# Dilated attention: the query's square sums behind three slabs, one group each, in place of all six among the scores

## What is computed

```python
q = (h @ w_q).reshape(bsz, seq, 3, 16, 64)
q = _rms(q, q_gain[:, None, :]) * 64 ** -0.5
...
s = jnp.einsum('birhd,bjrhd->bhrij', qb, kb) + biases[g]
s = jnp.where(valid, s, -jnp.inf)
```

## Time and profile before

| What | Value |
|---|---|
| Time, median of 3 runs | 2720.44 us (2717.47 to 2721.78) |
| The profiled execution | 2737.34 us |
| Its span in the trace | 2735.2 us |
| Mean granted clock of TensorE | 0.973 |
| TensorE busy (matmuls) | 2615.1 us, 96% |
| VectorE, ScalarE busy | 1762.1 us (64%), 1313.4 us (48%) |
| Dilated attention | about 2194 to 2535 us of the span |

### The profile page before, as it was taken

How to read it: one execution, slowest core, us unless ns; L and a number is a source line. 1 busy time by engine, 2 the same in 40 slices (tenths; PEclk the granted TensorE clock), 3 DMA queues, 4 the chain that set the end, 5 groups by cost and what they waited for, 6 DMA issues and landing times.

```text
span 2735.2 us, 60697 instructions
## 1 busy us (share of the span) xinstructions
PE 2615.1 (96%) x23300; PEld 2545.4 (93%) x23300; DVE 1762.1 (64%) x2831; ACT 1313.4 (48%) x1947; POOL 74.4 (3%) x106
## 2 busy tenths in 40 slices
PE   7997999899999999999989999699999999999999
PEld 7996887899999999989989998689999999999999
DVE  5657565566756757766657656867667565555774
ACT  5544433355545546555445445345555454454552
POOL 0000442000000000000000000000000000000000
PEclk9999997899999999999999999899999999999999
DMA  5554200344555655445545645126655564452564
GB/s 197 188 185 130 94 3 33 109 154 153 190 188 179 202 194 183 158 139 184 192 146 184 206 155 165 43 98 199 206 173 196 179 183 123 135 141 95 170 209 144
DMA packets 114321, 424.24 MB, mean 155 GB/s; under 512 B 12433, under 2 KB 19044, under 8 KB 113796
## 3 DMA queue, kind: packets, MB, share of 16 engines
q1 hardware_dynamic: 105696, 408.99, 45.3%
q10 hardware_dynamic: 8484, 13.30, 2.3%
HBM read 421.12 MB, written 1.12 MB: 154 GB/s over the span
## 4 chain that ended last, share of the span: by engine, by line
PE 91%; DVE 3%; ACT 2%; issue 2%; DMA 0%; ACTq 0%; POOL 0%; DVEq 0%; SPq 0%; POOLq 0%
PE bank L462 21%; PE bank L464 21%; PE bank L463 21%; PE bank L396 5%; PE bank L397 4%; PE bank L398 4%; PE bank L2186 2%; PE bank L1605 1%; ACT hi L339 1%; PE bank L1580 1%; PE bank L443 1%; PE bank L444 1%; PE bank L445 1%; PE bank L1189 1%; PE bank L2114 1%
## 5 line engine op out<-in xcount | busy, mean ns | idle before, releaser
L347 DVE TENSOR_TENSOR lo<-raw,hi 128x1024 fp32r<-128x1024 f32 (+1 forms) x728 | 936.6, 1294 | 419.8 <-ACT hi L339 418.2
L339 ACT ACTIVATE hi<-raw 128x1024 fp32r<-128x1024 f32 (+1 forms) x728 | 787.4, 1106 | 361.3 <-PE bank L398 184.2
L462 PE MATMUL bank<-Hh,hi 128*128 128x256 f32 x3120 | 875.9, 281 | 18.4 <-DVE lo L347 18.1
L463 PE MATMUL bank<-Hl,hi 128*128 128x256 f32 x3120 | 874.3, 280 | 0.0
L464 PE MATMUL bank<-Hh,lo 128*128 128x256 f32 x3120 | 874.3, 280 | 0.0
L462 PEld LDWEIGHTS bank<-Hh,hi 128*128 128x128 f32 x3120 | 591.7, 190 | 21.4 <-DVE lo L347 20.4
L463 PEld LDWEIGHTS bank<-Hl,hi 128*128 128x128 f32 x3120 | 592.2, 190 | 0.0
L464 PEld LDWEIGHTS bank<-Hh,lo 128*128 128x128 f32 x3120 | 590.1, 189 | 0.0
L464 PE MATMUL bank<-Ah,lo 128*128 128x256 f32 x1408 | 394.0, 280 | 0.0
L463 PE MATMUL bank<-Al,hi 128*128 128x256 f32 x1408 | 393.9, 280 | 0.0
L462 PE MATMUL bank<-Ah,hi 128*128 128x256 f32 x1408 | 393.9, 280 | 0.0
(11 more groups left out here) (414 smaller groups left out, 4164.5 us busy)
## 6 DMA issues: line engine op xcount, KB each, us to landing
raw<-in_w SPq DMA_DIRECT2D x600, 512.0 KB, 3.4
raw<-in_w SPq DMA_DIRECT2D x128, 704.0 KB, 4.2
dB<-dil_bias ACTq DMA_DIRECT2D x16, 384.0 KB, 10.0
X<-in_x SPq DMA_DIRECT2D x2, 512.0 KB, 5.3
mem_x<-in_mem ACTq DMA_DIRECT2D x1, 1024.0 KB, 4.7
gWS<-in_ws ACTq DMA_DIRECT2D x1, 1024.0 KB
gBS<-in_bs ACTq DMA_DIRECT2D x1, 1024.0 KB
out_x<-X SPq DMA_DIRECT2D x4, 256.0 KB, 2.6
```

Of the source, the lines that this page charges most:

```text
L339: act.activation(k.hi[:, q, :w], k.raw[:, q, :w], ACT.Copy).then_inc(k.hi_ready, 1)
L347: dve.tensor_tensor(k.lo[:, q, :w], k.raw[:, q, :w], k.hi[:, q, :w].bitcast(F32), ALU.subtract).then_inc(k.lo_ready, 1)
L462: pe.matmul(out, wh, xh, start=first, stop=False)
L463: pe.matmul(out, wh, xl, start=False, stop=False)
```

## The change

The sums leave the scores. A new method `pe_query_sums(pe, c, g)` runs the sums of one group, and is called behind q1 (i = 4) for group 0, behind q2 for group 1 and behind v0 for group 2, there in front of the even unit's scores. They are written to bank 3 from column 256 on, not from column 0. ScalarE squares each group by itself, behind its split at i = 3, 4 and 5, once VectorE has evicted that q slab; the square waits for the same group's sums of the pair before. TensorE waits for the square of the group that it sums, and for the key's scales in front of group 0. The query's scales wait for the sums of group 2.

```diff
--- before.py
+++ after.py
@@ -1497,8 +1497,10 @@
                     self.pe_transposes(pe, 2 * c - 1)
                 if c >= 2 and i == 5:
                     self.pe_heads(pe, c - 2)
+                if 4 <= i <= 6:
+                    self.pe_query_sums(pe, c, i - 4)
                 if i == 6:
-                    self.pe_scores(pe, 2 * c, sums=True)
+                    self.pe_scores(pe, 2 * c)
                 if c and i == 7:
                     self.pe_output(pe, 2 * c - 1)
 
@@ -1555,7 +1557,19 @@
                 ins = pe.transpose(out, self.VF[:, g, half * P:(half + 1) * P], k.ident)
         k.pe_done.done(ins, f"d.vt{c}")
 
-    def pe_scores(self, pe, u, sums=False):
+    def pe_query_sums(self, pe, c, g):
+
+        k = self.k
+        k.act_done.wait(pe, f"d.qsq{c}.{g}")
+        if g == 0:
+            k.act_done.wait(pe, f"d.rk{c}")
+        for half in range(2):
+            at = T + 2 * (GROUPS * half + g)
+            ins = pe.matmul(k.bank[3][:, at:at + 2], self.QSQ[:, g, (1 - half) * P:(2 - half) * P], k.sel[:, 0:2],
+                            start=True, stop=True)
+        k.pe_done.done(ins, f"d.qs{c}.{g}")
+
+    def pe_scores(self, pe, u):
 
         k, c, e = self.k, u // 2, u % 2
         k.dve_done.wait(pe, f"d.k{c}")
@@ -1565,18 +1579,8 @@
         else:
             pe.wait_ge(k.rstd_ready, self.sh.norm_n["pe"])
         f, z = slice(e * HEAD, (e + 1) * HEAD), c % 2
-        if sums:
-            k.act_done.wait(pe, f"d.qsq{c}")
-            k.act_done.wait(pe, f"d.rk{c}")
         for g in range(GROUPS):
             b, o = 4 + g // 2, (g % 2) * T
-            if sums:
-                for half in range(2):
-                    at = 2 * (GROUPS * half + g)
-                    ins = pe.matmul(k.bank[3][:, at:at + 2], self.QSQ[:, g, (1 - half) * P:(2 - half) * P], k.sel[:, 0:2],
-                                    start=True, stop=True)
-                if g == GROUPS - 1:
-                    k.pe_done.done(ins, f"d.qs{c}")
             pe.matmul(k.bank[b][:, o:o + T], self.Q[z][f, g, :P], self.K[z][f, g, :], start=True, stop=True)
             ins = pe.matmul(k.bank[6][:, g * P:(g + 1) * P], self.Q[z][f, g, P:], self.K[z][f, g, :P], start=True, stop=True)
         k.pe_done.done(ins, f"d.s{u}")
@@ -1651,9 +1655,11 @@
                     self.act_load(act, c + 1)
                 if c and i == 4:
                     self.act_probabilities(act, 2 * c - 1)
-                if i == 5:
-                    k.dve_done.wait(act, f"d.qraw{c}")
-                    d(act.activation(self.QSQ[:], self.Q[c % 2][:], ACT.Square), f"d.qsq{c}")
+                if x == "q":
+                    act.wait_ge(k.banks_freed, RING + s + 1)
+                    if c:
+                        k.pe_done.wait(act, f"d.qs{c - 1}.{g}")
+                    d(act.activation(self.QSQ[:, g, :], self.Q[c % 2][:, g, :], ACT.Square), f"d.qsq{c}.{g}")
                 if c >= 2 and i == 5:
                     self.act_heads(act, c - 2)
                 if i == 6:
@@ -1692,9 +1698,9 @@
     def act_query_scales(self, act, c):
 
         k = self.k
-        k.pe_done.wait(act, f"d.qs{c}")
+        k.pe_done.wait(act, f"d.qs{c}.{GROUPS - 1}")
         r = self.RQ[:, c % 2].rearrange("p h g e -> p (h g e)")
-        k.act_done.done(act.activation(r, k.bank[3][:, :12], ACT.Ln, bias=k.col(C_EPS), scale=1.0 / HEAD), f"d.lq{c}")
+        k.act_done.done(act.activation(r, k.bank[3][:, T:T + 12], ACT.Ln, bias=k.col(C_EPS), scale=1.0 / HEAD), f"d.lq{c}")
         k.act_done.wait(act, f"d.lq{c}")
         k.act_done.done(act.activation(r, r, ACT.Exp, scale=-0.5), f"d.rq{c}")
```

## The result

Over 19 runs of each kernel the median is 2704.03 us with the change and 2715.24 us without. The ratio of the times is 0.993, 95% interval 0.9909 to 0.995, so the change is worth 19 us (13.6 to 24.7) of 2715. (The two medians alone lie 11.2 us apart, under that interval; why they differ from the ratio the record doesn't show.) I had forecast 15.2. The median lies in my range; the ratio on 2715.24 gives 2696.2, just under its lower end. Of the 9.0 us between that and my 2705.2, 3.8 are a larger gain than forecast and 5.2 a lower start: I had built on 2720.44, the median of three runs.

What follows compares the result with a forecast made beforehand. The prediction took TensorE to bound the kernel, busy for 2615.1 of 2735.2 us. Its terms, -13.0 - 3.0 + 0.8 = -15.2 us, took the median 2720.44 to 2705.2 us, range 2698 to 2714.

Steps and rivals of the forecast that it cites:

- What bounds, and the cause of the fall: TensorE sets the pace; its clock halves behind even units' scores because of the long mixture of sums and scores, 4.16 us.
- Rival A: At the scores, the clock doesn't hang on the sums: all falls stay, 2718.2 us, chance 0.10; in part, 0.05.
- Rival B: Behind q1's slab, transposes meeting sums bring new falls in 7 pairs, making it slower: 2729.5 us, chance 0.05.
- C: Rival: TensorE gains, but VectorE or ScalarE becomes late and eats it; no chance of its own, counted in the width.
- (1) Clock: Behind the even units' scores the clock stays at 2.4 GHz, saving 13.0 us, bounds none to 13.6 us.
- 27.2 us are eight of them: Half-clock time behind the scores counted as eight pieces of 3.4 us, each costing 1.62 us, 13.0 us in all.
- The start of the sum: Forecast counted from the runs' median 2720.44 us, taking off the same 15.2 us as from the profiled execution.
- (2) Moved sums: Sums between slabs take 0.54 us a group, saving 0.38 us a pair, 3.0 us in all, bounds 0 to 3.0.
- (3) Squares: ScalarE's three squares for one cost it 3.4 us in all, hidden under its waits for TensorE: taken as zero.
- (5): Sums written to columns 256 to 267 of bank 3 add no instruction and cost nothing.
- (4) The wait in pair 0: TensorE waits some 0.8 us once for the square of q0 behind two DMA issues, bounds 0 to 1.0 us.

Runs made afterwards that it cites:

- e2_wide: Kernel before, order kept, each sum with a moving operand of 128 columns instead of 2: no fall, dilated attention 332.3 us, whole time 0.9979.
- e6_triple: Changed kernel with group 0's sums done three times over behind the transposes of q1: dilated attention 336.6 us, one fall, in pair 0.
- e8_after: Changed kernel, nothing altered, profiled once more: dilated attention 329.0 us with one window at half clock, whole time 0.9933 of the kernel before.
- e1_block: Kernel before with a pair's six sums in one block in front of the even unit's scores: five windows, dilated attention 333.2 us, whole time 0.9967.
- e12_squares: Kernel before with three squares of 256 columns for one of 768, sums still among the scores: dilated attention 340.5 us, seven windows at half clock.
- e7_before: Kernel before, nothing altered, profiled a second time: dilated attention 350.2 us with 12 windows of 3.4 us at half clock.
- e5_twogroups: Changed kernel with group 0's sums behind q2, groups 1 and 2 in front of the even unit's scores: dilated attention 326.4 us, one fall.

## Why the prediction was right or wrong

**What bounds, and the cause of the fall: right.** The falls at the scores went with the sums, and e2_wide shows that without sums of few columns there is none. Why twelve such loads bring it beside scores and not behind transposes (e6_triple) stays open. Rival A is out: none stays at the scores. By the rule of the Trainium skill (TensorE: Matmul & The Clock Gate, HAM oscillation — how this bites in real kernels), gaps in which TensorE is idle make it fall. The piece behind the wait of 2.1 us in pair 0 of e8_after goes that way, though the page speaks of longer gaps, and a wait of 1.9 us in the first profile brought none. Those of the earlier trace rows don't agree, since they stand behind 3.50 of 3.50 us busy. Rival B is out too (e6_triple): the transposes that the same page of the Trainium skill (Part 4: PE-mode transpose) says don't engage the full clock didn't lose it here, with sums behind them. So is C: no new wait of TensorE but that for the square of q0.

**(1) Clock: the step that failed.** The price of a window holds roughly: with 1.62 us each, four profiles of the kernel before come to between 328.9 and 329.8 us, once the 1.0 us of wait is taken off one. (I had read it against pair 1. Against pair 3 of the changed kernel, where the same slab takes from 2291.64 to 2294.58, 2.94 us, it is 1.53; between pairs of e1_block it is 1.7.) What failed is "27.2 us are eight of them". I read the number off one execution, and allowed 2 us either way. Four have 8, 12, 11 and 11 windows. The mean of 10.5 makes the term 17.0 us, not 13.0: 4.0 us too little, outside the 2 that I had allowed.

**The start of the sum: too high.** "I put the same difference on the median" set the time on the 2720.44 us of three runs; 19 gave 2715.24. These 5.2 us are no part of the change, and more than the 3.8 by which the gain was missed. Either miss alone stays inside my range: 2715.24 - 15.2 is 2700.0, and 2720.44 - 19 is 2701.4.

**(2) Moved sums: too small a gain.** I took 0.54 us for a group between slabs and noted that no row showed it. It is 0.44 to 0.45 for the groups behind slab or transposes, 0.54 in front of scores: 1.43 us a pair instead of 2.00. That is 0.57 us a pair and 4.6 us in all, against my 3.0. The lengths without falls and waits, 329.3 and 325.2 us, give 4.1. At 1.7 us a window they would give 3.3 and the clock 17.9, so between the two terms some 0.9 us can't be placed.

**(3) Squares: right,** by e12_squares. **(5)** needed no correction.

**(4) The wait in pair 0: too small.** 1.9, 2.1 and 2.6 us in three profiles, outside my 0 to 1.0. I took the duration of the DMA issues from the one trace (1.78 us). In these three profiles they took 2.95, 3.30 and 3.68 us, but the change isn't what lengthens them: they took 3.24 in e7_before, and 1.70 to 1.84 in eight profiles, e5_twogroups among them. What sets it stays open. Twice in three times the wait brought a fall of its own. I hadn't priced that.

The sum of what was measured: -17.0 - 4.1 + 2.0 (wait) + 0.8 (half a fall) = -18.3 us, against 18.5 between the profiles' means; the terms are taken from the same profiles, so this only shows that none is missing. Whole times gave 19 us, with a width of 5 us either way, so that this lies so close is luck in part.

## What to carry to other kernels

A stretch in which TensorE is always busy can still cost its clock, if many of its matmuls move only a few columns: look at the granted clock right behind such stretches, and spread them among dense matmuls or let them move more columns. What a window at half clock costs varies little (1.5 to 1.7 us here), but how many there are varies from one execution to the next; take several profiles before a term of a sum counts them. And an instruction that another engine now waits for should not stand behind DMA issues, whose duration is not steady (1.7 to 3.7 us for the same two).

## What was unexpected of the hardware

The spread of whole times (2680.8 to 2724.4 us for one kernel) must lie largely outside the dilated attention, where two things differ from profile to profile. One is the falls of the clock: between 88 and 139 us at half clock outside this stage in the fourteen profiles. The other is that a slab's matmuls follow each other in one of two rhythms at the same granted clock, whole stages long, and differently in each execution. The window from 700 to 740 us, in a feed-forward layer, of the kernel before:

```profile
700.00:740.00 40.00, 40.00 (x342) 40.00 (x341) 28.54 (x46) 20.35 (x29) 0.00 (x0) 1.00 0.56 185
```

and of the kernel after:

```profile
700.00:740.00 40.00, 40.00 (x355) 40.00 (x354) 28.02 (x43) 22.18 (x31) 0.00 (x0) 1.00 0.65 214
```

342 matmuls against 355 in 40 us, both at clock 1.00: 117 against 113 ns from one to the next. Counting distances of 116 to 122 ns in the trace, outside the falls, the first profile of the kernel before has some 10,300 and e7_before some 5,000; with the change there are 2,700 and, in e8_after, 8,600. So it isn't the change's doing. Between the first two profiles it makes 7,600 matmuls of some 4.5 ns, 34 of the 56.5 us. Falls make up the rest: over the whole span 150 us at half clock against 102, and half of the difference is 24. What sets the rhythm stays open.
